# A fused encoder layer: memory tokens transposed and column vectors gathered on the host, the memory norm applied to keys and values in PSUM

## The reference

```python
def rmsnorm(x, g):
    y = x * lax.rsqrt(jnp.mean(x * x, axis=-1, keepdims=True) + EPS)
    return y * g

def memory_cross_attention(xn, memn, w_xq, w_xkv, w_xo):
    q = (xn @ w_xq).reshape(B, S, 4, 256)
    kv = memn @ w_xkv                       # 256 x 2048: keys and values
    k, v = kv[..., :1024], kv[..., 1024:]   # each in 4 heads of 256
    s = einsum('bshd,bmhd->bhsm', q, k) * 256 ** -0.5
    p = softmax(s)
    return einsum('bhsm,bmhd->bshd', p, v) @ w_xo

# one layer
xn = rmsnorm(x, norm_mix_pre);  h = xn @ w_in
mix = concat(gated_linear_attention(h), spatial_gating(h)) @ w_out
x = x + rmsnorm(mix, norm_mix_post)
xa = memory_cross_attention(rmsnorm(x, norm_x_pre), rmsnorm(mem, norm_mem), w_xq, w_xkv, w_xo)
x = x + rmsnorm(xa, norm_x_post)
x = x + rmsnorm(swiglu(rmsnorm(x, norm_ffn_pre)), norm_ffn_post)
```

## Time and profile before

| | us |
|---|---|
| median of three executions | 1343.41 |
| the profiled execution, whole | 1340.38 |
| its span, first to last instruction | 1338.7 |
| PE busy | 1286.4 (96% of the span) |
| DVE busy | 737.2 (55%) |
| ACT busy | 544.3 (41%) |
| POOL busy | 216.2 (16%) |

### The profile page before, as it was taken

The page is one execution under the profiler, slowest core; times in us unless marked ns, Lnnn a source line. Parts: engine busy times, 40 slices in busy tenths (PEclk is TensorE's granted clock), DMA queues, the critical chain, the costliest instruction groups (busy, mean ns, idle before and its releaser), DMA issues.

```text
span 1338.7 us, 16987 instructions
## 1 busy us (share of the span) xinstructions
PE 1286.4 (96%) x6409; PEld 1076.2 (80%) x6409; DVE 737.2 (55%) x1111; ACT 544.3 (41%) x1022; POOL 216.2 (16%) x340
## 2 busy tenths in 40 slices
PE   6988999999999999999988999999999999999995
PEld 6986898778888888888867888888888887888874
DVE  4663331346443564455597666766676655454557
ACT  5876132342222453344454333333333333444343
POOL 1222000111000220002100000002455544000003
PEclk9999999999999999999999999999999999999998
DMA  6868221111133111212124554655444457786663
GB/s 237 266 233 259 71 64 47 33 32 47 64 105 112 36 48 47 64 45 85 44 79 160 194 197 181 211 190 181 150 173 173 165 197 252 226 282 183 204 203 127
DMA packets 73040, 189.70 MB, mean 142 GB/s; under 512 B 9152, under 2 KB 9728, under 8 KB 71552
## 3 DMA queue, kind: packets, MB, share of 16 engines
q1 hardware_dynamic: 61392, 151.35, 34.1%
q0 software_dynamic: 11520, 37.27, 7.6%
q10 hardware_dynamic: 48, 0.01, 0.0%
HBM read 137.22 MB, written 51.38 MB: 141 GB/s over the span
## 4 chain that ended last, share of the span: by engine, by line
PE 85%; DVE 5%; DMA 4%; ACT 2%; issue 2%; POOL 1%; DVEq 0%; SPq 0%; ACTq 0%; POOLq 0%
PE ps L1498 27%; PE ps L1500 27%; PE ps L1499 27%; PE ps L1523 2%; DMA wraw<-down_sums 1%; DMA output_weights<-stage 1%; POOL rstd L694 1%; DMA tok<-in_x 1%; DVE w_lo L483 1%; ACT ps L790 1%; PE ps L1597 1%; ACT w_hi L474 0%; POOL var L691 0%; DMA wsT<-in_b_spatial 0%; DVE last_lo L1293 0%
## 5 line engine op out<-in xcount | busy, mean ns | idle before, releaser
L1498 PE MATMUL ps<-w_hi,act_hi 128*128 128x512 f32 (+1 forms) x704 | 273.4, 388 | 0.0
L1500 PE MATMUL ps<-w_hi,act_lo 128*128 128x512 f32 (+1 forms) x704 | 267.7, 380 | 0.0
L1499 PE MATMUL ps<-w_lo,act_hi 128*128 128x512 f32 (+1 forms) x704 | 267.4, 380 | 0.0
L1500 PEld LDWEIGHTS ps<-w_hi,act_lo 128*128 128x128 f32 x704 | 132.4, 188 | 25.4
L1498 PEld LDWEIGHTS ps<-w_hi,act_hi 128*128 128x128 f32 x704 | 132.5, 188 | 25.1 <-issue 1.5
L1499 PEld LDWEIGHTS ps<-w_lo,act_hi 128*128 128x128 f32 x704 | 132.6, 188 | 23.7
L1499 PE MATMUL ps<-act_lo,w_hi 128*128 128x512 f32 x384 | 149.9, 390 | 0.0
L1288 DVE TENSOR_TENSOR w_lo<-wraw,w_hi 128x512 fp32r<-128x512 f32 x132 | 98.4, 748 | 87.5 <-ACT w_hi L918 87.5
L1498 PE MATMUL ps<-sums_hi,w_hi 128*128 128x512 f32 x352 | 137.9, 392 | 6.0 <-ACT spare L955 4.0
L1500 PE MATMUL ps<-sums_hi,w_lo 128*128 128x512 f32 x352 | 137.4, 390 | 0.0
L1293 DVE TENSOR_TENSOR w_lo<-wraw,w_hi 128x1024 fp32r<-128x1024 f32 x66 | 83.2, 1264 | 93.8 <-ACT w_hi L928 93.8
(11 more groups left out here) (234 smaller groups left out, 2158.8 us busy)
## 6 DMA issues: line engine op xcount, KB each, us to landing
wraw<-in_w_ffn_gu SPq DMA_DIRECT2D x44, 512.0 KB, 4.3
ffn<-in_w_ffn_down SPq DMA_DIRECT2D x22, 512.0 KB, 4.3
hidden_a<-ffn POOLq DMA_DIRECT2D x44, 256.0 KB, 3.3
down_sums<-ffn SPq DMA_DIRECT2D x11, 1024.0 KB, 3.8
hidden_s<-ffn POOLq DMA_DIRECT2D x44, 256.0 KB, 2.3
wraw<-hidden_s SPq DMA_DIRECT2D x44, 256.0 KB, 2.9
...
raw<-in_w_in SPq DMA_DIRECT2D x20, 512.0 KB, 3.7
```

Source lines behind the costliest of these rows:

```text
L1498: nc.tensor.matmul(out_, lh, rh, start=first, stop=False, skip_group_check=onto)
L1499: nc.tensor.matmul(out_, lh, rl, start=False, stop=False, skip_group_check=onto)
L1500: return nc.tensor.matmul(out_, ll, rh, start=False, stop=last, skip_group_check=onto)
```

## The change

The host now passes `mem` a second time, transposed (`mem_t`), and the five vectors as one array of 32 columns (`gains`). On the core:

- The transposed memory tokens are loaded unscaled in two halves of 512 KB (`memT_raw`, in the place of `act_hi`, free at that time). ACT copies each half to `memT_hi`, DVE subtracts to `memT_lo`. The 16 transposes of `mem` and the transpose of the vectors are gone; `columns` is one DMA of ACT.
- `mem` itself is still loaded, for the sums of squares only, behind two pieces of weights.
- The factors `rstd` of the 256 tokens are spread over columns by DVE (two instructions), transposed by PE before its step 2, and copied by DVE to `mem_rows`, a tile in which every partition holds the 256 factors.
- Each of the 16 evacuations of an `xk` or `xv` step gets a third link: DVE multiplies the PSUM bank by `mem_rows` in place, and only then may ACT read it (`kv_scaled` in place of `mm_done`).
- The DMAs of the first two tiles of `x` wait until ACT has squared the tile of `mem` that lies in the buffer, no longer for PE's transposes.

The diff, cut to its core:

```diff
@@ -145,7 +144,6 @@
     TR_AT = {n: [] for n in range(len(STEPS) + LAG)}
-    TR_AT[SNO["xk", 0, 0]] += [("mem", 0), ("mem", 1)]
     for t in range(TT):
@@ -525,12 +519,19 @@
             def x_in(t):
-                sp.wait_ge(tr_done, TRNO[("mem", t) if t < 2 else ("x", t - 2)] + 1)
+                if t < 2:
+                    sp.wait_ge(squared, squares(("mem", t)))
+                else:
+                    sp.wait_ge(tr_done, TRNO["x", t - 2] + 1)
                 sp.dma_start(tok[:, t % 2, :], xd[t]).then_inc(tok_landed[t % 2], 16)
 
-            for t in range(MT):
-                sp.dma_start(tok[:, t, :], memd[t]).then_inc(tok_landed[t], 16)
-            for p in range(NPIECE):
+            for h in range(2):
+                sp.dma_start(memT_raw[:, 4 * h:4 * h + 4, :], mem_t[:, 4 * h:4 * h + 4, :]).then_inc(mem_landed[h], 16)
+                piece(h)
+            sp.dma_start(tok[:, 0, :], memd[0]).then_inc(tok_landed[0], 16)
+            piece(2)
+            sp.dma_start(tok[:, 1, :], memd[1]).then_inc(tok_landed[1], 16)
+            for p in range(3, NPIECE):
                 if p in X_BEFORE:
@@ -652,9 +653,6 @@
                 pool.wait_ge(pool_own, own[0])
-
-            for v in VECTORS[3:]:
-                pool.dma_start(*vector_rows(v)).then_inc(rows_landed_pool, 16)
 
@@ -774,8 +772,7 @@
 
-            for v in VECTORS[:3]:
-                act.dma_start(*vector_rows(v)).then_inc(rows_landed, 16)
+            act.dma_start(columns[:, :], gains).then_inc(columns_landed, 16)
             JUNK = ps[:, Z, :]
@@ -828,7 +825,7 @@
                 if p == 0:
-                    act.wait_ge(columns_ready, 1)
+                    act.wait_ge(columns_landed, 16)
                 landed(act, p)
@@ -836,7 +833,7 @@
                 if kind in ("xk", "xv"):
-                    act.wait_ge(mm_done, n + 1)
+                    act.wait_ge(kv_scaled, 4 * b + t + (KT if kind == "xv" else 0) + 1)
                     f = 4 * b + t + (KT if kind == "xv" else 0)
@@ -982,22 +979,22 @@
 
+            for h in range(2):
+                act.wait_ge(mem_landed[h], 16)
+                nc.scalar.activation(memT_hi[:, 4 * h:4 * h + 4, :], memT_raw[:, 4 * h:4 * h + 4, :],
+                                     ACT.Copy).then_inc(mem_hi, 1)
+                split(h)
+            split(2)
+            split(3)
             in_square(("mem", 0))
             in_square(("mem", 1))
-            split(0)
-            tr_evac(("mem", 0))
-            split(1)
-            tr_evac(("mem", 1))
-            split(2)
-            split(3)
             for n in range(len(STEPS)):
...
                 for g in TR_AT[n]:
-                    if g[0] != "mem":
-                        tr_evac(g)
+                    tr_evac(g)
                 if n > 0 and STEPS[n - 1] == ("a", 0, 1):
@@ -1152,6 +1149,8 @@
                     f = 4 * b + t + (KT if kind == "xv" else 0)
+                    dve.wait_ge(mm_done, n + 1)
+                    nc.vector.tensor_tensor(bank(n, NM), bank(n, NM), mem_rows, ALU.mult).then_inc(kv_scaled, 1)
                     dve.wait_ge(kv_hi_done, f + 1)
@@ -1368,17 +1367,24 @@
 
-            dve.wait_ge(rows_turned, 1)
-            nc.vector.tensor_copy(columns[:, :], ps[:, O, 0:NVEC]).then_inc(columns_ready, 1)
-            dve.wait_ge(columns_ready, 1)
-            xh(("mem", 0))
-            xh(("mem", 1))
-            split(0)
-            tr_evac(("mem", 0))
-            tr_evac(("mem", 1))
-            split(1)
+            dve.wait_ge(columns_landed, 16)
+            for h in range(2):
+                dve.wait_ge(mem_hi, h + 1)
+                dve.wait_ge(mem_landed[h], 16)
+                hs = slice(4 * h, 4 * h + 4)
+                nc.vector.tensor_tensor(memT_lo[:, hs, :], memT_raw[:, hs, :], memT_hi[:, hs, :].bitcast(F32),
+                                        ALU.subtract).then_inc(mem_lo, 1)
+                split(h)
             split(2)
             split(3)
+            dve.wait_ge(consts, 1)
+            for t in range(MT):
+                dve.wait_ge(rstd_ready, JNO["mem", t] + 1)
+                nc.vector.tensor_scalar(mem_cols[:, t, :], ident[:, :], 0.0, rstd[:, JNO["mem", t] % 4, 0:1],
+                                        ALU.mult, ALU.add).then_inc(mem_cols_ready, 1)
+            dve.wait_ge(mem_rows_turned, 1)
+            nc.vector.tensor_copy(mem_rows, ps[:, O, 0:NM]).then_inc(mem_rows_ready, 1)
+            dve.wait_ge(mem_rows_ready, 1)
             for n in range(len(STEPS)):
@@ -1538,9 +1541,6 @@
             pe.wait_ge(consts, 1)
-            pe.wait_ge(rows_landed, 16 * 3)
-            pe.wait_ge(rows_landed_pool, 16 * (len(VECTORS) - 3))
-            nc.tensor.transpose(ps[:, O, 0:NVEC], vec_rows, ident[0:NVEC, 0:NVEC]).then_inc(rows_turned, 1)
             for n, (kind, b, t) in enumerate(STEPS):
@@ -1600,9 +1600,14 @@
                 if kind in ("xk", "xv"):
-                    if t == 0 and b == 0 and kind == "xk":
-                        pe.wait_ge(tr_lo, 2 * (TRNO["mem", 1] + 1))
+                    if n == 2:
+                        pe.wait_ge(mem_cols_ready, MT)
+                        for m in range(MT):
+                            ins = nc.tensor.transpose(ps[:, O, m * P:(m + 1) * P], mem_cols[:, m, :], ident[:, :])
+                        ins.then_inc(mem_rows_turned, 1)
                     for k in range(KT):
+                        if n == 0 and k % 4 == 0:
+                            pe.wait_ge(mem_lo, k // 4 + 1)
                         if t == 0 and k % 2 == 0:
@@ -1774,6 +1778,12 @@
     arrays, args = {}, []
+    inputs = dict(inputs)
+
+    a = inputs["mem"][0]
+    inputs["mem_t"] = a.T.reshape(a.shape[1] // 128, 128, a.shape[0]).transpose(1, 0, 2)
+    inputs["gains"] = _np.concatenate([inputs[name].reshape(-1, 128) for name in (
+        "norm_mem", "norm_mix_pre", "norm_x_pre", "gla_onorm", "b_spatial")]).T
     for name in _INS:
...
         if name == "w_xq":

```

More of the change, by code:

```diff
@@ L43, with build @@
 RING = 8
-def build(nc, x, mem, norm_mix_pre, w_in, w_gate_up, b_gate, gla_onorm, sg_ln_g, sg_ln_b,
-          w_spatial, b_spatial, w_out, norm_mix_post, norm_x_pre, norm_mem, w_xq, w_xkv,
-          w_xo, norm_x_post, norm_ffn_pre, w_ffn_gu, w_ffn_down, norm_ffn_post, out):
+def build(nc, x, mem, mem_t, gains, w_in, w_gate_up, b_gate, sg_ln_g, sg_ln_b,
+          w_spatial, w_out, norm_mix_post, w_xq, w_xkv, w_xo, norm_x_post, norm_ffn_pre, w_ffn_gu, w_ffn_down, norm_ffn_post, out):
     _, T, D = x.shape
@@ L193, in squares @@
         return sum(j[0] != "ln" for j in JOBS[:JNO[job] + 1])
-    XHS = [("mem", 0), ("mem", 1)] + [(n, t) for n in ("x", "xn2", "xn3") for t in range(TT)]
+    XHS = [(n, t) for n in ("x", "xn2", "xn3") for t in range(TT)]
     XHNO = {g: n for n, g in enumerate(XHS)}
@@ L252, in build @@
         decay = little("decay", [P, TT, 4])
-        VECTORS = [("mem", norm_mem, KT), ("mix", norm_mix_pre, KT), ("x", norm_x_pre, KT),
-                   ("gla", gla_onorm, HEADS), ("bsp", b_spatial, HEADS)]
-        NVEC = sum(v[2] for v in VECTORS)
+        VECTORS = [("mem", KT), ("mix", KT), ("x", KT), ("gla", HEADS), ("bsp", HEADS)]
+        NVEC = sum(w for _, w in VECTORS)
         columns = little("columns", [P, NVEC])
-        vec_rows = wsT[0:NVEC, 0, :]
+        mem_cols, mem_rows = wsT[:, 0:2, :], wsT[:, 2:4, :].rearrange("p a b -> p (a b)")
         pre, o = {}, 0
-        for name, _, w in VECTORS:
+        for name, w in VECTORS:
             pre[name] = columns[:, o:o + w]
@@ L492, in slot_free @@
                 eng.wait_ge(mm_done, LAST[p // 4 - 2] + 1)
-        def vector_rows(vector):
-            o = sum(v[2] for v in VECTORS[:VECTORS.index(vector)])
-            _, v, w = vector
-            return wsT[o:o + w, 0, :], v[0] if len(v.shape) == 3 else v.rearrange("o (k p) -> (o k) p", p=P)
         block = ctx.enter_context(nc.Block())
```

28 lines of the change are left out of this document (12 added, 16 removed).

## The result

| | before | after |
|---|---|---|
| median, us | 1343.04 (13 to 18 runs in later groups: 1342.99 to 1343.26) | 1357.93 (4 runs, 1356.53 to 1363.8) |
| ratio to before | | 1.0123, 95% interval 1.0102 to 1.0143 |
| the profiled execution, us | 1340.38 | 1356.53 |
| its span, us, and mean granted clock of PE | 1338.7, 0.995 | 1354.8, 0.986 |

The changed kernel is slower by 14.9 us on the medians and by 16.2 us on the two profiled executions. The forecast was 1362, or +18.4 on the profiled execution.

The account below looks back on a forecast made before the run. PE's waits in the first 126 us were taken as the bound, PE being busy nearly without a break afterwards. Stage delays 15.4 plus clock 3.0 gave 18.4 on 1340.4, 1358.8; the median 3.0 higher, 1362, range 1352 to 1370.

Parts of the forecast that it names:

- The opening, step 0: Start of the kernel: PE starts near 8.8 us instead of 15.6 and ends step 0 at 19.0 instead of 20.7.
- `mem_rows` and the first multiplication: In `xk 0`: copy done at 24.4 us, piece 4 landed about 22.9, first multiplication at 25.5 after DVE's split.
- The ring: In `xk` and `xv` steps: multiplication, `kv_hi`, `w_hi`, `w_lo`, next multiplication, nothing overlapped; 2.94 us, longer with `x` or transposed tiles.
- The multiplication: DVE's third link in each `xk` and `xv` evacuation: 0.42 us, bounds 0.2 and 0.75, all sixteen in the chain.
- The stages: Delay from late multiplications and rings: `xk 0` +5.1, `xk 1` +4.3, `xv 0` and `xv 1` +6.0; sum +15.4 us.
- The clock: PE runs at half clock behind long waits after `xk 0`, `xk 1` and `xv 1`: 3.0 us, ends 0 and 7.
- a late start is carried on one to one: In `xq` and `xo`, stages start from PE and their DMAs, stores and splits follow, so delays pass on in full.
- Rival 1: ACT and DVE close no ring; stage ends grow 0.5 us each, 1.5 in all; 1341 to 1345, chance 0.06.
- Rival 2: PE's earlier start wins, with the third link hidden as Rival 1 needs; about 1340 us, chance 0.05.
- Rival 3: Only rings holding a tile of `x` count, plus `xk 0`'s late first multiplication (2.8); about +9, 1352 us, chance 0.17.

Follow-up runs that it names:

- filler: The changed kernel with 44 extra matmuls that nobody reads on PE before `xq 0` and before `xq 1`; 1357.41 us.
- values_rows: The changed kernel with the values' factor moved from the `xv` evacuations to ACT's evacuation of `xo`, the keys keeping the multiplication; 1358.74 us.
- double: The changed kernel with a second multiplication of the bank, by 1.0, ahead of the first; 1366.59 us.
- no_link_fill: no_link with 28 matmuls never read before `xq 0`, before `xq 1` and before the `w_lo` wait in `xv 1`'s first step; 1348.64 us.
- no_link: The changed kernel without the multiplication, so keys and values lack the memory tokens' factors; 1347.46 us.
- no_link_x: no_link with the first two tiles of `x` requested before pieces 7 and 8 instead of 4 and 5; 1348.85 us.
- late_tok: The changed kernel with its factors moved to the `xo` and `xq` evacuations, and the tiles of `mem` requested behind piece 3; 1348.49 us.
- folded_x: The changed kernel with factors moved to the `xo` and `xq` evacuations, and the first two `x` tiles requested before pieces 7 and 8; 1345.87 us.
- link_only: The kernel before with only the third link added, multiplying by a tile of ones; 1355.75 us.

## Why the prediction was right, point by point

**Right in sign, mechanism and size.** +18.4 was forecast on the profiled execution and +16.2 measured; on the medians +14.9.

**The opening, step 0.** Forecast: last six matmuls begin behind a split done at 17.7, end at 19.0. Measured: they begin at 18.18, and step 1 begins at 19.62, 0.6 late. PE's first matmul was at 10.45, not 8.8: the split of piece 0 finished later than I had it. This did not matter, since all four groups of six matmuls wait for a piece.

**`mem_rows` and the first multiplication.** Forecast 24.4 for the copy, 22.9 for piece 4, 25.5 for the first multiplication. Measured: the copy ends at 25.1, the piece lands at 23.00, and the first multiplication is at 26.25. The last is 0.75 late because the copy is 0.7 late, and the copy because PE took up the transposes at 24.23 where I had 23.6: step 0 ended 0.6 later. Step 1 took 4.6 us, as forecast; 18 of its 24 matmuls were 0.21 us apart and the last ones 0.12. (For the opening this spacing is the reading to go by: the clock column of a window there shows 1.00 in both kernels, but the first record of the clock stands only where the spacing falls, at 23.6 us in after and 20.7 before.) The forecast gave no working for the landing at 22.9; that it came at 23.00 may be luck.

**The ring.** Forecast 2.94 us, measured 2.97. In `xk 1` forecast 4.98, 3.9 and 4.98 us, measured 4.90, 4.01 and 4.96 (multiplications at 55.47, 60.37, 64.38 and 69.34). In `xv` forecast 28.5 for seven rings, measured 92.00 to 121.12 in the chain, 29.1. The chain of waits of after goes through these rings in all of `xk` and `xv`, and through no landing of `x`. That is in part luck: the third tile took 5.9 us to land there, and 8.1 to 9.9 in filler, values_rows and double, where it lengthened the step. The forecast had no term for it.

**The multiplication.** Between 0.2 and 0.75 I had taken 0.42, and it is 0.42, read from PSUM and written to PSUM in place.

**The stages.** `xk 0` +5.1 forecast, +5.9 measured; `xk 1` +4.3 against +4.4 (`xk 1` from its first matmul to `xq 1`: 19.41 us, before 15.04); `xv` +6.0 against +4.8 (35.00, before 30.24). Sum 15.4 against 15.1. In `xv` two errors offset each other: the rings are 0.6 us longer in sum than forecast, but the first multiplication comes 4.5 us behind the stage's first matmul, where `kv_lo` came 6.3 us behind it before and I had kept that place. And PE does not wait 3.4 us for the end of `xv 1`: it waits 3.95 us at 108.34 for `w_lo`, between `xv 0` and `xv 1`, and 2.04 us at the end.

**The clock: right in what happens, its price open.** The clock fell behind the waits, in four stretches (33.8 to 40.6, 67.9 to 74.8, 108.9 to 112.3, 122.6 to 126.0 us). `xq 0` is 1.2 us longer than before and `xq 1` 2.0, which with `xk` and `xv` makes the 18.3 us at `xo 0`. So the trace of after alone agrees with the 3.0. What of it reaches the end is not settled. Filler and no_link_fill, with the clock full, are not faster by what their runs can tell, 2 to 3 us, which is nearly all that I booked. In their traces the full clock did bring later work forward (the first multiplication of `xk 1` by 1.9 us in filler, `xq 1` by 1.3 and `xo 0` by 2.5 in no_link_fill), and most of that was then lost again, in filler the 1.9 us at a tile that landed late. That "a late start is carried on one to one" was too simple: a landing, or a store of `stage` that ACT waits for, can take in a shift of one or two microseconds. The Trainium skill describes in "TensorE: Matmul & The Clock Gate", section "HAM oscillation — how this bites in real kernels", bursts that are shorter than the waits between them and start each time at the slow clock. The windows of after agree on the slow start (0.50 behind a wait of 5.85 us), though the burst there, `xq 0` with 14.85 us, is longer than the wait. What such a start costs in the end no run here settles.

**What I missed.** The rest of the change, without the link, costs 4.4 us (no_link). My sum had for it only the late first multiplication of `xk 0`, 25.5 against 22.7, which is 2.8; the other 15.6 were the rings and the clock. Measured is 10.5 for the link when it is taken out of after, and 12.7 when it is put into before. So the link was put 3 to 5 us too high and the rest up to 1.6 too low, and errors of opposite sign helped the total. Shown of the rest: 1.4 us of `xq 0`'s late start in no_link come from the order in SP's list, since moving the two requests takes just this away; the time of no_link_x shows no gain from it. Excluded: the tiles of `mem` ahead of piece 3 (late_tok), and the clock as the cause of all 4.4 us (no_link_fill). Not settled: what the 4.4 us are. Tiles of `x` that land late are the rival that is left. The third and the eighth tile took 5.3 and 5.6 us before, and in no_link 7.4 and 7.6, in no_link_x 7.5 and 6.6, in folded_x 6.4 and 7.2, in no_link_fill 6.5 and 7.1. ACT waited for tiles 2.6 us before, and 6.0 in no_link, 5.2 in no_link_x, 5.0 in no_link_fill. Against it: these are single executions, that of before is a fast one, and its seventh tile took 8.4 us. The transfers have the same size and the same queue, and no run changed the landings alone.

**The rivals.** Rival 1 (link hidden) is refuted by link_only, +12.7 with nothing else changed. Rival 2 (the early start wins) needed it, and no_link, where it holds, is still slower than before. Rival 3 (only rings with a tile of `x` count) is refuted by `xq 0`, which starts 5.9 us late where that rival gives at most 2.8, and by double.
